# Streaming encoder layer on eight cores: the down projection by output halves with its weights loaded once, a first tile that begins with v, and the bf16 stores of the weights spread over five tiles

## What is computed

```python
xn = rmsnorm(x, g_pre_mix)
xa, ga, u, v, gates = split(xn @ w_in)                  # four parts of 1024, gates 2048
xc, conv_new = causal_conv(xa, conv_prev, conv_w, conv_b)    # width 4
hseq, h_last = rglru(xc, h0, ...)                       # two small gate maps, a = exp(..), mult = sqrt(1 - a*a), scan
o_a = (hseq * gelu(ga)) @ w_br_a
vn  = layernorm(gelu(v), ln_g, ln_b)
o_b = (gelu(u) * spatial_gate(vn, w_s, b_s)) @ w_br_b   # 128x128 matrix per group, over positions
g_a, g_b = split(sigmoid(gates))
x = x + rmsnorm((g_a * o_a + g_b * o_b) @ w_out, g_post_mix)
gate, up = split(rmsnorm(x, g_pre_ffn) @ w_ffn_in)      # 2 x 2816
x = x + rmsnorm((silu(gate) * up) @ w_ffn_out, g_post_ffn)
```

## Time and profile before

| | |
|---|---|
| three timed runs | 2175.6, 2175.12, 2171.39 us, median 2175.12 |
| the profiled execution | 2172.2 us |
| its span, first to last instruction, slowest core (core 4) | 2170.7 us |
| spans of the eight cores | 2157.4 to 2170.7 us |
| mean granted PE clock of the eight cores | 0.983 to 0.987 of full speed |
| busy, share of the span | PE 95%, DVE 52%, ACT 45%, POOL 23% |
| chain that ended last | PE 81%, DMA 9%, ACT 3%, issue 3%, DVE 2%, POOL 1% |
| transfers | 443.03 MB counted at the destination, 204 GB/s; HBM read 468.14 MB, written 53.54 MB |

### The profile page before, as it was taken

How to read it: one execution, slowest core, us unless ns; L and a number is a source line. 1 busy time by engine, 2 the same in 40 slices (tenths; PEclk the granted TensorE clock), 3 DMA queues, 4 the chain that set the end, 5 groups by cost and what they waited for, 6 DMA issues and landing times.

```text
span 2170.7 us, 36559 instructions; the slowest of 8 cores (2157.4 to 2170.7 us)
## 1 busy us (share of the span) xinstructions
PE 2062.5 (95%) x10711; PEld 956.7 (44%) x10711; DVE 1125.8 (52%) x1569; ACT 971.6 (45%) x1528; POOL 504.0 (23%) x824
## 2 busy tenths in 40 slices
PE   4679999998999999999999999999999999999998
PEld 2235445434444444444444444444444444444543
DVE  4482776215683267623774167822676247742542
...
GB/s 174 206 175 197 175 169 150 163 231 268 243 192 177 219 275 184 180 205 273 247 216 259 194 258 240 145 155 228 272 182 148 172 240 250 154 149 210 191 166 234
DMA packets 197519, 443.03 MB, mean 204 GB/s; under 512 B 23120, under 2 KB 23184, under 8 KB 197328
## 3 DMA queue, kind: packets, MB, share of 16 engines
...
HBM read 468.14 MB, written 53.54 MB: 240 GB/s over the span
## 4 chain that ended last, share of the span: by engine, by line
PE 81%; DMA 9%; ACT 3%; issue 3%; DVE 2%; POOL 1%; SPq 0%; ACTq 0%; POOLq 0%; DVEq 0%
PE ps L567 80%; DMA mring<-wsc 3%; DMA fring<-wt 2%; DMA xpre<-xp 2%; DMA fring<-wsc 1%; PE ps L771 1%; ACT junk L573 1%; ACT L573 1%; DMA xres<-xp 1%; POOL stats L662 1%; DVE xres L798 0%; POOL stats L659 0%; ACT EE L573 0%; DVE XC L870 0%; DVE tokm L789 0%
## 5 line engine op out<-in xcount | busy, mean ns | idle before, releaser
L567 PE MATMUL ps<-hnT,fring 128*128 128x512 bf16 (+2 forms) x2880 | 629.0, 374 | 1.8 <-ACT sgt L573 0.9
L567 PE MATMUL ps<-xnT,mring 128*128 128x512 bf16 x2400 | 568.8, 383 | 16.3 <-ACT T L573 5.7
L567 PEld LDWEIGHTS ps<-hnT,fring 128*128 128x128 bf16 x2880 | 278.5, 98 | 330.6 <-issue 4.3
L573 ACT ACTIVATE T<-ps 128x512 f32<-128x512 f32 x259 | 152.2, 597 | 567.5 <-PE ps L567 549.2
L567 PEld LDWEIGHTS ps<-xnT,mring 128*128 128x128 bf16 x2400 | 231.0, 99 | 285.7 <-issue 30.4
L567 PE MATMUL ps<-fring,ffT 128*128 128x512 bf16 (+1 forms) x1416 | 341.8, 380 | 8.7 <-DMA fring<-wt 4.9
L1092 DVE SCALAR_TENSOR_TENSOR T<-T,ps 128x512 f32<-128x512 f32 x130 | 89.1, 687 | 354.6 <-PE ps L567 354.6
L1254 DVE SCALAR_TENSOR_TENSOR sgt<-sgt,ps 128x512 f32<-128x512 f32 (+2 forms) x182 | 122.6, 674 | 246.7 <-ACT sgt L573 243.8
L573 ACT ACT_TABLE_LOAD x167 | 214.3, 1283 | 35.1 <-PE ps L567 26.4
L567 PEld LDWEIGHTS ps<-fring,ffT 128*128 128x128 bf16 (+1 forms) x1416 | 135.6, 98 | 170.6 <-issue 18.9
L573 ACT ACTIVATE sgt<-ps 128x512 f32<-128x512 f32 (+2 forms) x182 | 107.1, 589 | 221.0 <-PE ps L567 201.1
(11 more groups left out here) (135 smaller groups left out, 1997.8 us busy)
## 6 DMA issues: line engine op xcount, KB each, us to landing
...
fring<-wt POOLq DMA_DIRECT2D x95, 512.0 KB, 9.3
mring<-wt POOLq DMA_DIRECT2D x58, 512.0 KB, 8.4
wsc<-fring SPq DMA_DIRECT2D x49, 512.0 KB, 10.5
xres<-xp SPq DMA_DIRECT2D x31, 512.0 KB, 10.1
yp<-xres SPq DMA_DIRECT2D x31, 512.0 KB, 6.5
xpre<-xp SPq DMA_DIRECT2D x29, 512.0 KB, 9.5
```

Source lines behind the costliest of these rows:

```text
L567: P.op("pe", lambda e: e.matmul(out, lhsT=lhsT, rhs=rhs, start=start, stop=stop), reads=reads, writes=writes, cost=max(27.0, n / 2.4 + 2.5))
L573: P.op("act", lambda e: e.activation(out=out, in_=in_, func=func, **kw), reads=reads, writes=writes, cost=165.0 + 0.833 * n + 93.0 * aps + ...
```

## The change

- **Down projection.** `s_fout(p, j)` now takes p as an output half. `w_ffn_out` is laid out so that a block holds 512 output channels of two rows of blocks (`wfo`); each p goes through 11 blocks, 8 matmuls of 512 columns per block and 2 to each of 4 banks (4 subtiles), in tile 0's FFN a fifth for the sample rows. `s_final(0)` squares and scales the first halves into `sgt` and `tokf`, `s_final(1)` does the second halves in place in PSUM and adds both halves to the residual.
- **Keys and banks.** `FFN_SPAN` is 0.82; pool `a` has 5 banks, `s` 3. W_OUT goes through `fring` in tiles 1 to 7.
- **Stores.** `STORE_AT`: FO at 1, the FFN's first 6 pairs at 2, the next 8 at 3, the last 8 at 4, gate A and branch A at 1, the rest as before. Pairs of the gates and branches are now two neighbouring blocks of one matrix.
- **First tile.** v comes first, all four subtiles and the sample rows under one load of its weights (`s_v0`); casts are released one by one by the four input rows (`gate`); then xa is mixed with u, the spatial matrices, ga and the first blocks of gate B and branch B. The loop over c calls `s_gb` and `s_ob` for blocks 0 to 3, and behind it they are called for blocks 2 and 3 again, with the same result (PE's list has 10775 matmuls, before 10711: 32 more of 512 columns and 32 of 64); the sample's gates are evacuated in quarters. In other tiles the gate and branch units go two by two.
- The planner's cost of a transferred byte is 310 instead of 300 per ns.

The diff, cut to its core (the bodies of the first tile's v, a re-cut of `s_v`, and the evacuations of the sample's gates are left out):

```diff
-FFN_SPAN = 0.92
+FFN_SPAN = 0.82
...
-POOLS = dict(a=(0, 1, 2, 3), s=(4, 5, 6, 7))
+POOLS = dict(a=(0, 1, 2, 3, 4), s=(5, 6, 7))
...
-         + [(g + m, r + m) for g, r in ((W_GTA, W_BRA), (W_GTB, W_BRB)) for m in range(8)]
-         + [(W_OUT + c, W_OUT + c + 1) for c in range(0, 8, 2)]
+         + [(b + c, b + c + 1) for b in (W_GTA, W_GTB, W_BRA, W_BRB, W_OUT) for c in range(0, 8, 2)]
...
 def STORE_AT(q):
     pid = PAIRS[q][0]
-    if W_GTB <= pid < W_BRA:
-        return 3
-    if W_U <= pid < W_V:
+    if W_FG <= pid < W_FO:
+        j = pid - W_FG
+        return 2 if j < 6 else 3 if j < 14 else 4
+    if pid >= W_FO:
+        return 1
+    if pid < W_U or W_V <= pid < W_GTA or W_OUT <= pid < W_FG:
+        return 0
+    if pid < W_V:
         return 4
-    if W_FG <= pid < W_FG + 11:
+    if pid < W_GTB or W_BRA <= pid < W_BRB:
         return 1
-    if W_FG + 11 <= pid < W_FO:
+    if pid < W_OUT:
         return 3
     return 0
...
-                        self.open[q] = self.load_pair(q, u == at, () if pid == W_XA else first_rows[:1]) if u <= at else None
+                        self.open[q] = self.load_pair(q, u == at, gate()) if u <= at else None
...
+            def gate():
+                n = min(n_casts[0], NSUB)
+                n_casts[0] += 1
+                return first_rows[n - 1:n] if n else ()
...
-                        S["wo"] = [mr.get(W_OUT + k) for k in range(NCH)]
+                        S["wo"] = [(fr if i else mr).get(W_OUT + k) for k in range(NCH)]
...
+                def pair_of(fn, m):
+                    for x in (m, m + 1):
+                        add(U, lambda x=x: fn(x))
+
...
+                    for h in range(2):
+                        for s in range(NSUB + 1):
+                            add(U, lambda h=h, s=s: s_v0(h, s))
+                        if h == 0:
+                            add(0, gate_constants)
+                    for c in range(NCH):
+                        add(U, lambda c=c: s_xa(c))
+                        if c == 0:
+                            add(0, gate_loads)
+                            add(0, row_loads)
+                            add(0, row_sums)
+                        if c >= 1:
+                            add(0.43, lambda c=c: s_gate(c - 1))
+                        if c < 4:
+                            u_sp(2 * c)
+                        else:
+                            pair_of(s_gb if c % 2 == 0 else s_ob, 2 * (c // 2 - 2))
+                        if c % 2 == 0 and c >= 2:
+                            a_tail(c - 2)
+                        if c < 4:
+                            u_sp(2 * c + 1)
+                        if c == 2:
+                            add(0, s_vs_out)
+                        if c == 4:
+                            add(0.5, s_sampU)
+                    add(0.43, lambda: s_gate(7))
+                    a_tail(6)
+                    pair_of(s_gb, 2)
                     add(0.5, s_sampA)
-                for g in range(8):
-                    add(U, lambda g=g: s_u(g))
-                    add(0.25, lambda g=g: s_sp(g))
-                if samp:
-                    add(0.5, s_sampU)
-                for m in range(NCH):
-                    add(U, lambda m=m: s_gb(m))
-                    if samp and m == 2:
-                        add(0, late_loads)
-                    add(U, lambda m=m: s_ob(m))
-                    add(U, lambda m=m: s_gA(m))
-                    add(U, lambda m=m: s_oa(m))
-                if samp:
+                    pair_of(s_ob, 2)
+                    add(0, late_loads)
+                    for m in (0, 2):
+                        pair_of(s_gA, m)
+                        pair_of(s_oa, m)
+                    for m in (4, 6):
+                        for fn in (s_gb, s_ob, s_gA, s_oa):
+                            pair_of(fn, m)
                     add(0, s_sampM)
+                else:
+                    vu = [(0, 0), (0, 1), (1, 0), (1, 1)]
+                    for c in range(NCH):
+                        add(U, lambda c=c: s_xa(c))
+                        if c % 2 == 0:
+                            add(2 * U, lambda c=c: s_v(*vu[c // 2]))
+                        if c >= 1:
+                            add(0.43, lambda c=c: s_gate(c - 1))
+                        if c % 2 == 0 and c >= 2:
+                            a_tail(c - 2)
+                    add(0.43, lambda: s_gate(7))
+                    a_tail(6)
+                    for g in range(8):
+                        u_sp(g)
+                    for m in range(0, NCH, 2):
+                        for fn in (s_gb, s_ob, s_gA, s_oa):
+                            pair_of(fn, m)
                 if i + 1 < NT:
                     for s in range(NSUB):
                         add(0.45, lambda s=s: prep_sub(i + 1, s, P.key - (0.10 if s < 2 else 0.0)))
```

```diff
                 def s_fout(p, j):
                     if j == 0:
-                        S["fo"] = [fbank() for _ in range(4)]
-                        if samp and p == 0:
-                            S["fos"] = [fbank() for _ in range(2)]
-                    got = [fr.get(W_FO + jj) for jj in range(j, j + (NLAST if j == NFF - NLAST else 1))]
-                    for ss in range(2) if len(got) > 1 else (None,):
+                        S["fo", p] = [fbank() for _ in range(NSUB)]
+                        if samp:
+                            S["fos", p] = fbank()
+                    got = [fr.get(W_FO + NFH * p + jj) for jj in range(j, j + (NLAST if j == NFH - NLAST else 1))]
...
-                                if samp and p == 0 and ss != 1:
-                                    for h in range(2):
...
+                                for u in range(2):
+                                    f = 2 * jj + u
+                                    mm(512, ps[0:PT, b, :], lhs_of(f), w[:, u * 512:(u + 1) * 512], f == 0, f == NFF - 1,
+                                       [cell] + reads(f), [("ps", b)])
+
+                    for s in range(NSUB):
+                        unit(128, S["fo", p][s], lambda f: ffT[:, f, s * 128:(s + 1) * 128], lambda f: [("ffT", f)])
+                    if samp:
+                        unit(64, S["fos", p], lambda f: ffT_s[:, f, :], lambda f: [("ffT_s", f)])
...
                 def s_final(p):
...
+                    for s in range(NSUB):
+                        b = S["fo", p][s]
+                        tk, tc = (sgt[:, s, :], ("sgt", s)) if s < 2 else (tokf[:, (s - 2) * 512:(s - 1) * 512], ("tokf", s - 2))
+                        q = stat()
+                        act(512, junk[:, p * 512:(p + 1) * 512], ps[:, b, :], AF.Square, [("ps", b)], [("st", q)],
+                            chain="junk", accum=stats[:, q:q + 1], scale=1.0 / 32.0)
+                        if p == 0:
+                            S["q0", s] = q
+                            dve(512, lambda e, tk=tk, b=b: e.tensor_tensor(out=tk, in0=ps[:, b, :], in1=gbc_pf[:, 0:512], op=ALU.mult),
+                                [("ps", b), ("gbc_pf",)], [tc])
+                            continue
+                        q0 = S["q0", s]
                         xb, xc, _, ysem = xbuf(i, s)
                         if owner[xc] != (i, s):
                             raise ValueError(f"{xc} belongs to {owner[xc]}")
                         owner[xc] = None
-                        alt = i == NT - 1 and s == NSUB - 1
-                        post_norm(S["fo"][2 * ss:2 * ss + 2], 128, xb, xc, gbc_pf, "gbc_pf", EPS, *((tokm, "tokm") if alt else (tokf, "tokf")))
+                        dve(512, lambda e, b=b: e.tensor_tensor(out=ps[:, b, :], in0=ps[:, b, :], in1=gbc_pf[:, 512:1024], op=ALU.mult),
+                            [("ps", b), ("gbc_pf",)], [("ps", b)])
+                        r = rstd_from(stats[:, q0:q0 + 1], 128, stats[:, q:q + 1], EPS, [("st", q0), ("st", q)], op0=ALU.add)
+                        for h, (src, sc) in enumerate(((tk, tc), (ps[:, b, :], ("ps", b)))):
+                            dve(512, lambda e, h=h, src=src, xb=xb, r=r: e.scalar_tensor_tensor(
+                                out=xb[:, h * 512:(h + 1) * 512], in0=src, scalar=stats[:, r:r + 1], in1=xb[:, h * 512:(h + 1) * 512],
+                                op0=ALU.mult, op1=ALU.add), [sc, ("st", r), xc], [xc])
                         r0 = (i % TPS) * TT + s * 128
                         P.op("sp", lambda e, xb=xb, r0=r0: e.dma_start(out=yp[i // TPS, r0:r0 + 128, :], in_=xb),
                              reads=[xc], dma_sem=ysem, serial=True, cost=70.0, nbytes=1 << 19)
...
+    wfo = g("w_ffn_out").reshape(NFH, 2, 128, 2, 512).transpose(3, 0, 2, 1, 4).reshape(NFF, 128, 1024)
```

213 lines of the change are left out of this document (110 added, 103 removed).

## The result

The changed kernel took 2141.9 us in the median of its runs (2140.6 at best), the kernel before on the same chip 2173.3; the ratio is 0.9857, with a 95% interval of 0.9838 to 0.9876. That is 31 us less, where 44 were forecast: faster by more than the 4.4 us that the prediction took for the least that can be told, inside the range, about 11 us above the predicted time. The profiled execution took 2143.0 us with a span of 2141.4 us on its slowest core, core 1, against 2172.2 and 2170.7 (core 4) before.

The account below looks back on a forecast made before the run. PE bounds 600 to 2120 us; open time lies in tile 0 and 425 to 600 us. Terms 8 + 3 - 33 - 13 - 4 - 5 = -44 us from 2172.2: 2128 profiled, 2131 us median, range 2102 to 2172.

Parts of the forecast that it names:

- The start: Before the first unit: two more casts share the transfer engines with the last input rows, +3 us (0 to 7).
- Tile 0: First unit to last branch A unit: v first frees PE from the gate chain; 65 us lost become 32, -33 us.
- 425 to 600 us: Tile 1's stretch: halved FO block loads and an earlier FFN end cut the loss from 25 to 12 us, -13.
- Tiles 2 to 7: Additional casts run beside a busy PE; -4 us of the 13 idle, bounds -13 and +15.
- Repeated units: Tile 0: gate B and branch B of blocks 2 and 3 done twice, 7.8 us of PE work, +8 us.
- the one on the span: Tile ends: with the FFN over at 0.86, nine units of the next tile's xa and v cover the output projection.
- the tile ends open: Rival: rows' chain uncovered at tile ends, 8 us at each of 7, 56 us, so 2187 us; chance 0.10.
- The end: Last down projection: loads keep up (-3 us), half left to square in the last subtile (-2 us); -5 us.
- The rival on the casts: Rival: 43 more casts in tiles 0 to 5 are the bound, -3 us in all, so 2172 us; chance 0.12.

Follow-up runs that it names:

- down_only: The kernel before with the new down projection, its layout, FFN span 0.82 and W_OUT in `fring`; first tile, pairs and stores as before: 0.9918 of before.
- first_only: The changed kernel with the down projection, its layout and store rule, FFN span (0.92) and W_OUT's ring as before: 1.0025 of before.

## Why the prediction was right, and where it was off

**The start** (+3): +1.2; the first v unit stands at 26.48, with 28 expected. From 29.30 on its matmuls run at the full rate (4 in 1.03 us), as forecast before 60 us; what the forecast did not have is the half clock from 66.83 to 76.9 us behind the wait for `Ti`.

**Tile 0** (-33): -41.5. The picture of ten v units without a gap, and of v and u as work that needs little of DVE, held: the last branch A unit ended at 192, with 202 forecast. Oversized was the loss to DVE's chain: 22 us for DVE and 6 for casts were in the sum, and PE waited 15.3 us in all from 25 to 160 us, 1.9 of them for a cast. (`RR` took 15.4 us to land, where the sum had the 12.4 of before.) But the term ended at the last branch A unit. The addition and the rows behind it, which the new order puts closer to the output projection, cost 6.4 us more; tile 0 as a whole gives 35 us, 27 with the repeated units counted.

**425 to 600 us** (-13): -14.1. What PE waited for there, against the earlier trace rows:

```profile
PE ps L786 <- ACT xsb L578: 3.9, 3, 2.4
PE ps L572 <- ACT xcb L578: 2.6, 1, 2.6
```

No cast and no block load is among them. down_only shows that this is the down projection's gain, and first_only that without it the casts of the new stores would have cost more than that. The forecast size was right, but in that sum 8 more pair casts against fewer loads are a small item of -6 us; without the fewer loads the new stores alone turned a loss of 28 us into 43 on the slowest core.

**Tiles 2 to 7** (-4): 0. From 600 to 950 us 11.5 us are lost instead of 2.7, from 950 to 2000 us 7.0 instead of 15.8. The first is almost all the end of tile 2, where the transfer engines are full (0.99) and PE waits for `xsb` and for a block, not for a cast. The casts and stores that the new rule leaves to tiles 2 and 3 are the likely cause; no run took them apart. (By the store rule tile 3 has 32 pair casts, not the 34 of the prediction: two of its pairs have one use more in tile 0. With 32 its terms add up to the 43.)

**Repeated units** (+8): 5 and 11 us by the two pairs of ratios, 7.9 by the medians beside each other, 7.8 by count.

**The step that failed** is the one on the span. The rival "the tile ends open" had the mechanism, rows of the chain and the price, 8 us per end, but it counted the seven ends behind which a next tile starts, and was held unlikely because that tile's units stand in the list to cover them. That holds at the ends of tiles 3 to 6, where PE waits 0.9 to 1.3 us, and not at tile 2's (7.6 us). Tile 7's end, the eighth, has no next tile; the prediction did not look at it by itself, and it cost the whole price and more, 10.4 us. With that end in the sum at the prediction's own 8 us the forecast would have been -36 for -29.

**The end** (-5): -1.2. The last matmuls and the last store, PE and SP's issues:

```profile
2093.07 38.15 PE L572 MATMUL ps<-fring,ffT 128*128 128x512 bf16 x176
...
2135.60 0.33 SPq L1398 DMA_DIRECT2D yp<-xpre  x1
```

The loads did keep up: 176 matmuls stand in one row without a wait. The last store is issued 4.4 us behind the last matmul, where it was 5.1 (2162.6 to 2167.65), so of the 2 us forecast for the chain 0.7 came. But the span ends 5.8 us behind that issue instead of 3.0. The likely reason, not tested: with halves of the output, all four subtiles are stored at the very end (four issues from 2130.26 on), and no longer two of them in the middle of the down projection.

**Luck.** That the time came within 11 us of the forecast is partly chance: tile 0's term gave 8.5 us more than forecast, and covered part of what tile 7's end (10.4), the wait behind tile 0 (6.4), tiles 2 to 7 (4) and the end (3.8) took. The rival on the casts had the right resource: it said a time near before's, and first_only, without the halved loads, has that. Its sum went by a transfer share of 0.87 in tile 0, where the earlier trace rows have 0.86 up to 160 us and 0.96 behind.
